# Sum of squares over the value columns of recurrent heads: fp32 matmuls replaced by single-pass matmuls on high and low parts

## The reference, cut to what matters

```python
def mixer_c(xn, S0, w_in, lb, norm_g, w_out):
    q, f, i, g = jnp.split(xn @ w_in, [C_DK_T, 2 * C_DK_T, 2 * C_DK_T + C_DV_T], axis=-1)
    ...
    o, S = gla_chunked(q..., k_in..., i..., log_f..., S0)
    o = rms_norm(o, norm_g).reshape(Bsz, L, C_DV_T) * jax.nn.silu(g.astype(f32))
    return o.astype(xn.dtype) @ w_out, S.astype(S0.dtype)
```

## Time and profile before

| | before |
|---|---|
| median of 3 runs | 1327.26 us (1327.24 to 1327.82) |
| profiled execution | 1327.69 us |
| its span, first to last instruction | 1325.9 us |
| mean granted TensorE clock | 0.999 |
| busy: PE / DVE / ACT / POOL | 1312.7 / 800.9 / 597.0 / 186.6 us |
| share of the chain that ended last: PE / DVE / ACT | 92% / 5% / 2% |

### The profile page before, as it was taken

One profiled execution on the slowest core, in us unless ns is written; L12 is line 12 of the kernel. 1 busy time (PEld: TensorE's weight loads), 2 busy tenths in 40 slices (PEclk: granted clock), 3 DMA queues, 4 the chain that ended last, 5 costly groups with the idle time before them and its releaser, 6 DMA issues.

```text
span 1325.9 us, 31859 instructions
## 1 busy us (share of the span) xinstructions
PE 1312.7 (99%) x12604; PEld 1281.6 (97%) x12604; DVE 800.9 (60%) x1458; ACT 597.0 (45%) x1211; POOL 186.6 (14%) x320
## 2 busy tenths in 40 slices
PE   9999999999999999999999999999999999999998
PEld 8998999999999999998999999999999999999998
DVE  6476576655655532228988888867565565552223
ACT  5367355433333322226766666656433333332232
POOL 0111121111111100000211111111111111120000
PEclk9999999999999999999999999999999999999999
DMA  8312231222223332213323333341123222332211
GB/s 293 115 50 64 80 97 49 95 95 82 92 80 95 106 107 88 81 49 89 115 97 106 104 97 97 98 136 58 53 90 95 91 83 80 100 123 88 87 44 68
DMA packets 39637, 123.23 MB, mean 93 GB/s; under 512 B 4184, under 2 KB 12120, under 8 KB 39448
## 3 DMA queue, kind: packets, MB, share of 16 engines
q1 hardware_dynamic: 34808, 111.37, 26.7%
q10 hardware_dynamic: 4592, 10.56, 2.3%
q0 software_dynamic: 176, 0.44, 0.1%
HBM read 113.78 MB, written 8.57 MB: 92 GB/s over the span
## 4 chain that ended last, share of the span: by engine, by line
PE 92%; DVE 5%; ACT 2%; issue 1%; DMA 0%; POOL 0%; SPq 0%; DVEq 0%; ACTq 0%
PE acc L453 85%; DVE w_lo L1423 1%; PE aux L803 1%; PE aux L748 1%; PE aux L610 1%; DMA raw<-in_w_in_ab 0%; DVE x L1645 0%; PE aux L831 0%; DVE mix L1640 0%; PE aux L531 0%; PE aux L632 0%; PE aux L622 0%; DVE h_lo L1432 0%; PE aux L549 0%; ACT pr L1007 0%
## 5 line engine op out<-in xcount | busy, mean ns | idle before, releaser
L1423 DVE TENSOR_TENSOR w_lo<-raw,w_hi 128x512 fp32r<-128x512 f32 (+1 forms) x372 | 305.5, 825 | 322.3 <-ACT w_hi L928 322.1
L453 PE MATMUL acc<-h_hi,w_hi 128*128 128x272 f32 x2208 | 474.5, 293 | 3.6 <-DVE h_lo L1432 2.5
L453 PE MATMUL acc<-h_hi,w_lo 128*128 128x272 f32 x2208 | 464.7, 288 | 0.0
L453 PE MATMUL acc<-h_lo,w_hi 128*128 128x272 f32 x2208 | 463.4, 288 | 0.0
L453 PEld LDWEIGHTS acc<-h_hi,w_hi 128*128 128x128 f32 x2208 | 349.6, 188 | 15.7 <-issue 7.5
L928 ACT CAST w_hi<-raw 128x512 fp32r<-128x512 f32 (+1 forms) x372 | 236.3, 642 | 264.7 <-PE acc L453 258.6
L453 PEld LDWEIGHTS acc<-h_lo,w_hi 128*128 128x128 f32 x2208 | 349.9, 189 | 0.2
L453 PEld LDWEIGHTS acc<-h_hi,w_lo 128*128 128x128 f32 x2208 | 347.9, 189 | 0.1
L453 PE MATMUL acc<-g_hi,w_hi 128*128 128x272 f32 x704 | 153.1, 288 | 0.0
L453 PE MATMUL acc<-g_hi,w_lo 128*128 128x272 f32 x704 | 153.0, 289 | 0.0
L453 PE MATMUL acc<-g_lo,w_hi 128*128 128x272 f32 x704 | 152.4, 288 | 0.0
(11 more groups left out here) (276 smaller groups left out, 1347.1 us busy)
## 6 DMA issues: line engine op xcount, KB each, us to landing
raw<-in_w_up SPq DMA_DIRECT2D x88, 512.0 KB, 3.6
raw<-in_w_down SPq DMA_DIRECT2D x32, 704.0 KB, 4.1
raw<-in_w_in_c SPq DMA_DIRECT2D x32, 512.0 KB, 3.6
raw<-in_w_in_ab SPq DMA_DIRECT2D x18, 512.0 KB, 3.7
raw<-in_w_out_ab SPq DMA_DIRECT2D x8, 512.0 KB, 3.6
S<-in_state ACTq DMA_DIRECT2D x8, 512.0 KB, 3.6
o_ss<-Snew ACTq DMA_DIRECT2D x8, 512.0 KB, 2.6
raw<-in_w_out_c SPq DMA_DIRECT2D x8, 512.0 KB, 3.6
```

The costliest lines, as they stand in the source:

```text
L453: mm = pe.matmul(acc[out][:, t, 0:H], w[slot][:, wc], mv[:, kk_, t * H:(t + 1) * H], start=start and k == 0 and q == 0, stop=stop and k == ...
L1423: dve.tensor_tensor(w_lo[slot][:, to], raw[n % 4][:, cols], w_hi[slot][:, to], ALU.subtract).then_inc(lo_ready, 1)
```

## The change

The squares in the scratch tile stay as they are. ScalarE now also copies them into a tile `osq_h` of type float32r (their high part, signal `osq_hi`), VectorE subtracts that from the squares into `osq_l` (`osq_lo`), and TensorE sums both parts with a float32r matrix of ones that POOL writes once: four single-pass matmuls in place of two fp32 ones. `osq_h` and `osq_l` lie on the place of the tiles `lev`, so VectorE waits for the finished sums before it writes the first level differences. In the last head's rest, VectorE's addition of the states goes ahead of the subtract.

```diff
+                    with ExitStack() as c:
+                        osq_h, osq_l = [sb(n, [P, T], F32R, c) for n in ("osq_h", "osq_l")]
                     lev = [sb(f"lev{i}", [P, TP], F32, b) for i in range(len(SPANS))]
...
+                    ones_r = sb("ones_r", [P, P], F32R, b)
...
                     if t == 4:
                         pe.wait_ge(C["snew_ready"], 2 * prev + 2)
-                        pe.wait_ge(C["osq_ready"], prev + 1)
-                        pe.matmul(A[0][:, 0:H], ones[:], S[2][:, 0:H], start=True, stop=True)
-                        pe.matmul(A[1][:, 0:H], ones[:], S[2][:, H:T], start=True, stop=True
-                                  ).then_inc(C["ostat_done"], 1)
+                        pe.wait_ge(set_up, 7)
+                        pe.wait_ge(C["osq_lo"], prev + 1)
+                        for z in range(2):
+                            pe.matmul(A[z][:, 0:H], ones_r[:], osq_h[:, cols(z)], start=True, stop=False)
+                            mm = pe.matmul(A[z][:, 0:H], ones_r[:], osq_l[:, cols(z)], start=False, stop=True)
+                        mm.then_inc(C["ostat_done"], 1)
...
                         act.activation(S[2][:, TP:T], A[2][:, TP // 2:TP // 2 + NB * TS], ACT.Square
                                        ).then_inc(C["osq_ready"], 1)
+                        act.wait_ge(C["osq_ready"], prev + 1)
+                        act.copy(osq_h[:], S[2][:]).then_inc(C["osq_hi"], 1)
...
                 if prev is not None and t == 3:
+                    if cur is None:
+                        state_added(prev)
+                    dve.wait_ge(C["osq_hi"], prev + 1)
+                    dve.tensor_tensor(osq_l[:], S[2][:], osq_h[:], ALU.subtract).then_inc(C["osq_lo"], 1)
                     if cur is not None:
                         kd_ops(cur)
                         diag_ops(cur)
-                    else:
-                        state_added(prev)
...
                 if t == 4:
+                    if prev is not None:
+                        dve.wait_ge(C["ostat_done"], prev + 1)
                     level_ops(0, cur)
                     level_ops(1, cur)
...
+            pool.memset(ones_r[:].bitcast(F32), 1.0).then_inc(set_up, 1)
```

More of the change, by code:

```diff
@@ L329, in build @@
                  "diag_ready", "al_done", "al_taken", "al_copied", "u_done", "us_done", "st_ready", "oc_done",
-                 "osq_ready", "ostat_done", "ors_ready", "og_ready", "oy_ready", "oy_hi", "oy_lo",
+                 "osq_ready", "osq_hi", "osq_lo", "ostat_done", "ors_ready", "og_ready", "oy_ready", "oy_hi", "oy_lo",
                  "kdT_done", "kdT_hi", "kdT_copied", "v_hi", "v_lo", "vcT_done", "vcT_copied", "vbd_ready", "gn_ready",
```

## The result

The changed kernel takes 1331.01 us (median of 7 runs, 1330.68 to 1333.91), the kernel before 1327.54 us in the same measurement: a ratio of 1.0029, 95% interval 1.0019 to 1.0039, so +3.47 us. It is slower, by what the sum had said (+3.5).

The account below looks back on a forecast made before the run. In the recurrent heads TensorE (31.63 us) barely outpaces a ScalarE-VectorE ring (31.40); the subtract makes the ring 32.04 and pacemaker. 3.10 + 0.25 + 0.13 = +3.5 us gives 1330.7 us, range 1328.4 to 1332.2.

Parts of the forecast that it names:

- the sum: Whole kernel: 3.10 + 0.25 + 0.13 = +3.5 us, giving 1330.7 on the median.
- the ring: Recurrent heads: ScalarE and VectorE waiting for each other, not TensorE; period 31.40 us a head against TensorE's 31.63.
- The ring takes the pace: Recurrent heads: ring grows to 32.04 us, TensorE needs 31.21 and idles 0.83 a head; chance 0.70.
- The subtract: VectorE, ahead of L1845, on the ring: 0.64 us a head, upper bound 0.73, lower bound zero.
- The copy is hidden: ScalarE, between squares and exponential of G: copy of about 0.65 us, covered by 2.78 us idle for kd.
- VectorE's second wait: VectorE, ahead of the level differences, waiting for the finished sums: cost zero.
- Four passes in 0.50: TensorE's sums: four single-pass matmuls take 0.50 us against 0.92, a gain of 0.42 a head.
- The transposes of head 7, +3.10: TensorE, head 7: seven subtracts, 4.48 us, less saved slack of 1.38, put its transposes 3.10 us later.
- The last head's rest, +0.25 and +0.13: TensorE, last head: level products stall about 0.25 us for VectorE's mask; sums 0.55 late less 0.42 saved, +0.13.
- Faster: Heads: subtract moves VectorE's L1952 off POOL's product, ring 30.89, TensorE keeps the pace, 1324.5 us; chance 0.08.
- No change: Heads: part of the subtract is absorbed, ring grows only 0.3 a head, +1.1 us, 1328.4; chance 0.17.
- The copy's wait: Heads: a second loop through TensorE, squares, copy, subtract, root and transposes binds; 0.3 beyond gives 1332.8 us; chance 0.05.

Follow-up runs that it names:

- the kernel with both moves: Changed kernel with POOL's second product held until VectorE's level differences and ScalarE's exponential of kd moved behind the root: 1325.57 us, ratio to the kernel before 0.9984.
- the differences earlier: Changed kernel with VectorE's state addition, subtract and kd differences put ahead of its accumulator evacuation and weight split: 1338.1 us, ratio to the kernel before 1.0077.
- the exponential behind the root alone: Changed kernel with ScalarE's exponential of kd moved behind the root, POOL left as it was: 1332.09 us, ratio 1.0034.

## Why the prediction was right, step by step

*The place to measure from.* The traces of before and after differ already ahead of the change. The same matmul in the first stage and just ahead of the heads, order of time on TensorE, in the kernel before:

```profile
20.51 0.62 PE L544 MATMUL aux<-scratch,ones 128*128 128x272 f32 x2
...
592.18 0.62 PE L544 MATMUL aux<-scratch,ones 128*128 128x272 f32 x2
```

and in the changed kernel:

```profile
19.82 0.62 PE L547 MATMUL aux<-scratch,ones 128*128 128x272 f32 x2
...
591.49 0.62 PE L547 MATMUL aux<-scratch,ones 128*128 128x272 f32 x2
```

The profiled execution of after stands 0.69 us ahead from its first 20 us on. The change isn't the reason: over the eleven traces of this case that row lies anywhere between 19.82 and 20.67, in kernels of either kind. The span of after is 3.0 us longer, so the heads and what follows cost 3.7; the sum said 3.48. That the medians differ by 3.47 is closer than the terms are, and to that extent luck.

The prediction misread one thing in the rows of the ring. It said that ScalarE and VectorE wait for each other and neither for TensorE. In the trace of before, ScalarE waits for TensorE twice in a head, for its squares and for a weight split. Order of time on ScalarE, that split behind the `kd` differences of head 1 and of head 5:

```profile
675.61 0.62 ACT L928 CAST w_hi<-raw 128x512 fp32r<-128x512 f32 x1 [0.49 <-PE acc L453]
...
802.11 0.62 ACT L928 CAST w_hi<-raw 128x512 fp32r<-128x512 f32 x1 [1.46 <-PE acc L453]
```

From head to head the wait is 0.49, 0.72, 0.97, 1.21, 1.46: it grows by 0.24, which is what the ring gains on TensorE in a head. Then it stays (1.48), because TensorE holds the ring: L1845 is 31.62 and 31.69 us apart in the last two heads, not 31.40. The 31.40 of the earlier trace rows is thus the ring's own period only because it was read over the heads ahead of this. The sum isn't touched, since the lengthened ring never catches TensorE up; in the changed kernel this wait stays at 0.6.

- *The ring takes the pace.* Its period is 32.03, where 32.04 was predicted. TensorE idles 0.79 us a head, where 0.83 was predicted, most of it at the transposes. Three kernels show it: the subtract alone costs nearly as much as the change, without the subtract the heads go at 31.38, and with the ring shortened elsewhere the loss goes.
- *The subtract* was priced at 0.64 and takes 0.63.
- *The copy is hidden:* the high part ends at 685.97 + 0.65 = 686.62 (predicted about 686.7), VectorE gets to the subtract at 687.66, and ScalarE still idles 2.69 for `kd`.
- *VectorE's second wait costs nothing:* L1818 at 692.71 starts with no idle time ahead of it.
- *Four passes in 0.50:* they start 0.13, 0.12 and 0.13 apart once they run. After a wait the first two are 0.20 apart (688.52, 688.72), so the four take 0.58 there, and a head's sums save 0.34 and not 0.42. Where TensorE didn't wait, in the kernel with both moves, the first two are 0.13 apart.
- *The transposes of head 7, +3.10:* 852.72 against 850.39 is 2.33, and with the 0.69 of the start 3.02.
- *The last head's rest, +0.25 and +0.13.* Order of time on TensorE and its weight loads, first before, then after (answers to the earlier trace rows):

```profile
862.26 0.22 PEld L738 LDWEIGHTS aux<-lev 128*32 128x32 f32 x16
```

```profile
864.80 0.22 PEld L741 LDWEIGHTS aux<-lev 128*32 128x32 f32 x13 [0.33 <-issue]
...
873.23 0.36 PE L853 MATMUL aux<-osq_h,ones_r 128*128 128x272 f32 x1 [0.45 <-DVE osq_l L1971]
```

  The level products start 864.80 - 862.26 + 0.69 = 3.23 later than before, 0.21 more than the transposes (0.25 predicted). The profile names no releaser for them; VectorE's mask result ends at 864.68, 0.12 ahead. TensorE's last product of the head (L787, at 870.55 against 867.83 before) starts 3.41 later, and the sums 873.23 - 869.90 + 0.69 = 4.02 later, where 3.10 + 0.25 + 0.55 = 3.90 was worked out. So the sums add 0.61 (0.55 predicted); the 0.45 in the row counts from the recorded end of the matmul ahead. The three terms are right to 0.1 each. The sum lacks 0.18 between the level products and L787: TensorE's products with the states (L770) take 0.88 from start to next start against 0.70 before, and why stays open.

The rivals. *Faster:* its mechanism is real and its condition wasn't met: L1959 stayed beside POOL at 1.87. When a wait parted the two, the changed kernel gained 4.0 us. The Trainium skill (SBUF — State Buffer, SBUF: two separate sides) says that a GpSimd operation and a VectorE one with two SBUF inputs take the port in turn, and the traces agree: 1.87 beside POOL, 0.72 apart from it. But parting them brought 31.37 a head and not 31.21. In that kernel the sums were there in time, but ScalarE's root stood behind the `kd` exponential, which waited 1.98 us for VectorE's differences, and TensorE's transposes waited for the root. The prediction had a loop through the root and the transposes, in its last rival, but not with the `kd` exponential on it; the kernel with the exponential behind the root, at 31.2, shows that this order of ScalarE was what was left. Which path closed that loop isn't shown. *No change:* nothing was absorbed, 32.03 - 31.40 = 0.63. *The copy's wait* is zero in the changed kernel; it binds, at 0.58 us a head, only where the differences were moved earlier.

My own failures lie in the experiments. Two of them (the differences earlier, the exponential behind the root alone) were computed from lists of work, and in both the move decided anew which VectorE operation stands beside POOL: two level differences in place of the product with the root. In the first the copy's wait came on top. That this is the whole of either miss wasn't tested.

Why does the kernel with both moves gain 1.9 us and not eight times 0.42? Its transposes of heads 1 and 7 are 187.25 us apart against 189.78 in the earlier trace rows: six heads at 0.42, all of it. Before head 1 and after head 7 it gains nothing and loses some 0.7 us of these 2.5, and one line of its table of waits over the heads says part of the reason:

```profile
PE aux L853 <- DVE osq_l L1978: 0.8, 2, 0.4
```

The two waits are those of the sums of the first and of the last head, where TensorE reaches them ahead of the low part. What else is lost wasn't followed and stays open.

## What to carry to other kernels

A share of 99% on one engine doesn't say that time taken off it is gained. Look, in the stage concerned, for a second clock: take an instruction of the other engines that never waits for the busy one, and read its period over several repetitions in which it isn't held. Here it was 31.40 against 31.63, so the whole margin was 0.23 us, and 0.64 us of work put on that ring cost more than 0.42 us off the busy engine brought.

Then work on the clock that sets the pace, and on the other only after it: moving a collision with POOL off the ring, onto an operation behind which VectorE used to idle, was worth nothing before the change and 4.0 us after it. Look where the collision goes: in two kernels here it went to operations that cost as much or more. And before comparing two traces by a stage's start, compare a row that lies ahead of the change.

## What the runs showed of the hardware

The price of standing beside POOL isn't a constant. Where VectorE works on two tiles beside POOL, its operation ends a fixed time after POOL's: in the changed kernel L1959 ends at 695.91 + 1.87 = 697.78, POOL's product at 695.32 + 1.88 = 697.20, 0.58 before it; 256 columns end 0.28 to 0.29 after POOL's in four cases (758.32 and 759.81 against 758.03 and 759.53; 763.05 and 764.55 against 762.77 and 764.27). 0.58 and 0.28 are nearly the whole operation (0.64 and 0.33 start to start). So in these traces VectorE's operation waits for the rest of POOL's and only then runs, whatever its own length, and a small one can be stretched most: 0.41 to 1.57. POOL pays in the same way when it comes second. Its 1.88 began at 695.32, 0.02 behind a weight split on VectorE (695.30, 0.69 long); where POOL came first and VectorE waited, it took its usual 1.36 (759.77 above). An evacuation isn't held up, in the order of time of the changed kernel:

```profile
693.67 1.69 POOL L2151 TENSOR_TENSOR c_E<-c_E,c_qn 128x544 f32<-128x544 f32 x1 [17.20 <-ACT c_E L1377]
694.05 0.71 DVE L1914 TENSOR_TENSOR c_vv<-acc,rstd 128x544 f32<-128x544 f32 x1
```

It reads an accumulator and runs its usual 0.71 in the middle of POOL's product. What to read for it is thus POOL's start and end, and the price is how much of POOL's operation is still to come when VectorE arrives.
